# Decode attention of a hybrid decoder step: scores kept as groups of 32 partitions, transposes by VectorE, keys in transfers of 1.25 MB

## What is computed

```python
k_all = concatenate([kv_buf[:, :, 0], k], axis=1)          # 2048 cached rows and the 8 new ones
for _, d in ((128, 1), (512, 4), (2048, 16)):              # window, dilation
    idx = w_buf + arange(t)[:, None] - arange(129)[None, :] * d
    s = einsum('bthd,btkhd->bthk', q, k_all[:, idx]) * HEAD_DIM ** -0.5
    lse = logsumexp(s, axis=-1)
    outs.append(einsum('bthk,btkhd->bthd', exp(s - lse[..., None]), v_all[:, idx]))
# the three branches are weighted by the softmax of their lse
```

## Time and profile before

| | before |
|---|---|
| median of the runs | 1509.22 us |
| the profiled execution, its own time | 1509.26 us |
| its span, first to last instruction | 1507.3 us |
| PE busy | 1494.9 us |
| DVE busy | 824.6 us |
| ACT busy | 584.6 us |
| moved by DMA | 296.59 MB, mean 197 GB/s |
| attention of the new tokens | about 141 to 490 us |

### The profile page before, as it was taken

One profiled execution on the slowest core, in us unless ns is written; L12 is line 12 of the kernel. 1 busy time (PEld: TensorE's weight loads), 2 busy tenths in 40 slices (PEclk: granted clock), 3 DMA queues, 4 the chain that ended last, 5 costly groups with the idle time before them and its releaser, 6 DMA issues.

```text
span 1507.3 us, 27167 instructions
## 1 busy us (share of the span) xinstructions
PE 1494.9 (99%) x11095; PEld 1414.1 (94%) x11095; DVE 824.6 (55%) x1075; ACT 584.6 (39%) x792; POOL 221.7 (15%) x316
## 2 busy tenths in 40 slices
PE   9999999999999999999999999999999999999997
PEld 9999777777778999999999999999999999999997
DVE  7669899964566677444444444444444433333434
ACT  6333434446545354333333333333333323333332
POOL 7874344500630000000000000000000000000100
PEclk9999999999999999999999999999999999999999
DMA  7557899999987444444444444444444444444442
GB/s 270 187 160 246 293 370 371 335 367 356 345 316 263 155 149 145 154 153 144 150 153 147 146 153 150 144 151 153 145 148 153 147 147 153 152 143 153 150 151 105
DMA packets 83282, 296.59 MB, mean 197 GB/s; under 512 B 9984, under 2 KB 11136, under 8 KB 82816
## 3 DMA queue, kind: packets, MB, share of 16 engines
q1 hardware_dynamic: 82624, 294.34, 57.6%
q10 hardware_dynamic: 576, 1.08, 0.2%
HBM read 289.31 MB, written 5.43 MB: 196 GB/s over the span
## 4 chain that ended last, share of the span: by engine, by line
PE 90%; DVE 5%; POOL 2%; issue 1%; ACT 1%; DMA 0%; DVEq 0%; ACTq 0%
PE ps L2001 20%; PE ps L2002 20%; PE ps L2000 20%; PE ps L1846 6%; PE ps L1884 3%; PE ps L1848 3%; PE ps L1890 2%; PE ps L1885 2%; PE ps L1658 2%; PE ps L1687 2%; DVE wlo L986 1%; PE ps L1952 1%; PE ps L1953 1%; PE ps L1951 1%; POOL par L1425 1%
## 5 line engine op out<-in xcount | busy, mean ns | idle before, releaser
L1300 DVE TENSOR_TENSOR wlo<-raw,whi 128x1024 fp32r<-128x1024 f32 x264 | 325.2, 1232 | 519.9 <-ACT whi L863 519.8
L863 ACT ACTIVATE whi<-raw 128x1024 fp32r<-128x1024 f32 x264 | 279.9, 1060 | 606.2 <-PE ps L2002 601.7
L2002 PE MATMUL ps<-xh,wlo 128*128 128x320 f32 x1400 | 432.6, 309 | 0.0
L2000 PE MATMUL ps<-xh,whi 128*128 128x320 f32 x1400 | 432.6, 309 | 0.0
L2001 PE MATMUL ps<-xl,whi 128*128 128x320 f32 x1400 | 432.6, 309 | 0.0
L2000 PEld LDWEIGHTS ps<-xh,whi 128*128 128x128 f32 x1400 | 262.8, 188 | 0.0
L2002 PEld LDWEIGHTS ps<-xh,wlo 128*128 128x128 f32 x1400 | 262.8, 188 | 0.0
L2001 PEld LDWEIGHTS ps<-xl,whi 128*128 128x128 f32 x1400 | 262.8, 188 | 0.0
L2000 PE MATMUL ps<-hh,whi 128*128 128x320 f32 x696 | 215.1, 309 | 0.0
L2001 PE MATMUL ps<-hl,whi 128*128 128x320 f32 x696 | 215.1, 309 | 0.0
L2002 PE MATMUL ps<-hh,wlo 128*128 128x320 f32 x696 | 215.1, 309 | 0.0
(11 more groups left out here) (335 smaller groups left out, 1804.1 us busy)
## 6 DMA issues: line engine op xcount, KB each, us to landing
raw<-in_w_gu SPq DMA_DIRECT2D x176, 512.0 KB, 3.5
raw<-in_w_dn SPq DMA_DIRECT2D x88, 512.0 KB, 3.5
raw<-in_w_in SPq DMA_DIRECT2D x78, 512.0 KB, 5.9
kv<-in_ck SPq DMA_DIRECT2D x76, 512.0 KB, 6.7
kv<-in_cv SPq DMA_DIRECT2D x64, 512.0 KB, 7.7
raw<-in_w_out SPq DMA_DIRECT2D x32, 512.0 KB, 3.7
raw<-in_cv SPq DMA_DIRECT2D x16, 512.0 KB, 7.7
out_kv<-z SPq DMA_DIRECT2D x2, 1280.0 KB, 12.4
```

Of the source, the lines that this page charges most:

```text
L863: act.activation(whi[:, j % SPL, :], raw[:, j % RAW, :], ACT.Copy).then_inc(S["w_hi"], 1)
L1300: v.tensor_tensor(wlo[:, j % SPL, :], raw[:, j % RAW, :], whi[:, j % SPL, :].bitcast(F32), ALU.subtract) \
L2000: t_.matmul(out, whi[:, slot, w], ah[:, k, :], start=(k == 0), stop=False)
L2002: last = t_.matmul(out, wlo[:, slot, w], ah[:, k, :], start=False, stop=(k == 2 * units - 1))
```

## The change

The scores of a pair of head groups are kept as four groups of 32 partitions: partition group j holds the keys 32 j to 32 j + 31 of every tile of 128, and the free axis runs over four pairs of head groups (`sall` is 128 x 4 x 352). Four score steps replace five, one for each pair, each with 8 products of 320 columns whose keys lie in runs of 32. The new keys go to one partition group (8 products of 32 columns in one column group), and a memset keeps the others masked.

The maximum of a query now lies over four partition groups: ACT copies them side by side (`spread_maxima`, four copies), DVE reduces (`maxima`), ACT copies the result back (`spread_bias`, four copies), and the exponent is four instructions of 352 columns. The sums over the partition groups come from four one-column products on PE (`sum_probabilities`, bank 6) and DVE inverts them. The transposes of 32 x 32 blocks are one instruction on DVE (`turn_probabilities`), two for the first two batches; PE's transposes and ACT's evictions are gone.

A pair's keys are one load of 1.25 MB with rows of 2 KB, and the ring is laid out by size. Each batch starts one slot later, its values one step and its output one step earlier. GpSimd clears `vn` once at the start. The core of the diff:

```diff
-KEY_TILES = (KEYS_OLD + 512) // P
-NKEYS = KEY_TILES * P + DEC_BATCH * DEC_SEQ
+KEYS = KEYS_OLD + 512
+KEY_TILES = KEYS // P
+KQ = KEYS // 4
+KW = KQ + 32
 KU = 2 * P
-KN = KEY_TILES * P // KU
+KN = KEYS // KU
+KS = 4
+K_PARTS = ((0, KN),)
+NP = len(K_PARTS)
...
-START_OF = (36, 42, 48, 54, 60, 66, 72, 78)
-TURN, VALUES, OUTPUT = 5, 7, 12
+START_OF = (37, 43, 49, 55, 61, 67, 73, 79)
+TURN, VALUES, OUTPUT = 5, 6, 11
...
-        kv = upper.take("kv", [P, KV - 1, ATT_WIDTH])
+        kv = upper.take("kv", [P, KV_ROOM])
         hb_more = upper.take("hb_more", [P, 2, NT])
-        sall = upper.take("sall", [P, NKEYS])
-        ptk = upper.take("ptk", [P, KEY_TILES + 1, P])
+        sall = upper.take("sall", [P, 4, KW])
+        ptk = upper.take("ptk", [P, 4, KW])
...
-            for b in batches(s, TURN + 1):
-                end.append((7, ("pt", b, 2)))
-            for step in range(KN):
+            for step in range(KS):
                 for b in batches(s, step):
                     end.append((6, ("score", b, step)))
+            for b in batches(s, TURN):
+                end.append((6, ("norm", b)))
...
-                    "pt": lambda: ("pt_moved", 4 * key[1] + (key[2] + 1 if key[2] < 2 else 4)),
-                    "score": lambda: ("s_masked", 6 * key[1] + (key[2] + 1 if key[2] < 4 else 6)),
+                    "score": lambda: ("s_masked", KS * key[1] + key[2] + 1) if key[2] < KS - 1 else ("new_masked", key[1] + 1),
+                    "norm": lambda: ("s_sum", key[1] + 1),
...
+        KV_FROM, KV_AFTER, held, in_raw, pos = [], [], [], None, 0
+        for n, (kind, _, i) in enumerate(KV_ORDER):
+            size = kv_size(kind, i)
+            if kind == "v" and (in_raw is None or n - in_raw >= KV - 1):
+                KV_FROM.append(None)
+                KV_AFTER.append([] if in_raw is None else [in_raw])
+                in_raw = n
+                continue
+            if pos + size > KV_ROOM:
+                pos = 0
+            KV_AFTER.append([m for m, lo, hi in held if lo < pos + size and hi > pos])
+            held = [x for x in held if x[0] not in KV_AFTER[n]] + [(n, pos, pos + size)]
+            KV_FROM.append(pos)
+            pos += size
+        KV_DONE = []
+        for n in range(len(KV_ORDER)):
+            KV_DONE.append(max([KV_DONE[n - 1] if n else -1] + KV_AFTER[n]))
...
+                if kind == "k":
+                    c0, c1 = K_PARTS[i % NP]
+                    src = a["ck"][KN * b + c0:KN * b + c1, :, 512 * (i // NP):512 * (i // NP) + 512].rearrange("c p n -> p c n")
+                    sy.dma_start(kv_place(n).rearrange("p (c n) -> p c n", n=512), src).then_inc(KV_IN[n % KV], 16)
+                else:
+                    sy.dma_start(kv_place(n), a["cv"][KEY_TILES * b + i, :, :]).then_inc(KV_IN[n % KV], 16)
...
+            def spread_maxima(b):
+                act.wait_ge(S["s_max"], b + 1)
+                for j in range(4):
+                    act.activation(quads[0:32, j, :], smax[32 * j:32 * j + 32, 0:4], ACT.Copy).then_inc(S["s_spread"], 1)
+            def spread_bias(b):
+                act.wait_ge(S["s_top"], b + 1)
+                for j in range(4):
+                    act.activation(sbias[32 * j:32 * j + 32, 0:4], sbias[0:32, 4:8], ACT.Copy, scale=-SCALE).then_inc(S["s_bias"], 1)
             def exponent(b):
-                act.wait_ge(S["s_max"], b + 1)
-                act.activation(sall[:], sall[:], ACT.Exp, bias=smax[:, 7:8], scale=SCALE, accum_out=rsum[:, 0, b:b + 1]).then_inc(S["p_exp"], 1)
-            def probabilities(b, g):
-                act.wait_ge(S["pt_done"], 3 * b + g + 1)
-                if g == 0 and b:
-                    act.wait_ge(S["v_used"], KEY_TILES * b)
-                bank, w = (7 if g else 6), (4 if g < 2 else 2)
-                new = g == 2 and b >= LATE
-                act.activation(ptk[:, 4 * g:4 * g + w + new, :].rearrange("p a n -> p (a n)"), ps[:, bank, 0:(w + new) * P], ACT.Copy) \
-                    .then_inc(S["pt_moved"], 1 + new)
-                if g == 2 and b < LATE:
-                    if b == 0:
-                        act.wait_ge(S["x_rot"], PAIRED)
-                    act.activation(ptk_late[b][:], ps[:, bank, 256:384], ACT.Copy).then_inc(S["pt_moved"], 1)
+                act.wait_ge(S["s_bias"], 4 * b + 4)
+                for g in range(4):
+                    act.activation(sall[:, g, :], sall[:, g, :], ACT.Exp, bias=sbias[:, g:g + 1], scale=SCALE,
+                                   accum_out=psums[:, b, g:g + 1]).then_inc(S["p_exp"], 1)
...
-                for b in batches(s, TURN):
-                    probabilities(b, 0)
-                    probabilities(b, 1)
...
                 for b in batches(s, 4):
+                    spread_maxima(b)
+                    spread_bias(b)
                     exponent(b)
...
-                dve.wait_ge(S["k_used"], KN * b + i + 1)
-                m = max(i - 2, 0) * KU
-                v.tensor_tensor_reduce(out=sall[:, KU * i:KU * i + KU], in0=ps[:, 6, 0:KU], in1=mask[:, m:m + KU], scale=1.0, scalar=-3e38,
+                dve.wait_ge(S["k_used"], KS * b + i + 1)
+                v.tensor_tensor_reduce(out=sall[:, i, 0:KQ], in0=ps[:, 6, 0:KQ], in1=mask[:], scale=1.0, scalar=-3e38,
                                        op0=ALU.add, op1=ALU.max, accum_out=smax[:, i:i + 1]).then_inc(S["s_masked"], 1)
-                if i < KN - 1:
+                if i < KS - 1:
                     return
-                new = 8 * (DEC_BATCH - 1 - b)
-                v.tensor_tensor_reduce(out=sall[:, KEY_TILES * P:NKEYS], in0=ps[:, 6, KU:KU + 64], in1=mask_new[:, new:new + 64], scale=1.0,
-                                       scalar=-3e38, op0=ALU.add, op1=ALU.max, accum_out=smax[:, 5:6]).then_inc(S["s_masked"], 1)
-                dve.wait_ge(S["s_masked"], 6 * b + 6)
-                step(v.tensor_reduce(smax[:, 6:7], smax[:, 0:6], AX.X, ALU.max))
-                v.tensor_scalar(smax[:, 7:8], smax[:, 6:7], -SCALE, None, ALU.mult).then_inc(S["s_max"], 1)
+                own = slice(32 * (b // 4), 32 * (b // 4) + 32)
+                at = 8 * (DEC_BATCH - 1 - b)
+                valid = mask_new[own, at:at + 32].rearrange("p (a n) -> p a n", a=1).to_broadcast([32, 4, 32])
+                fresh = sall[own, :, KQ:KW]
+                if b:
+                    dve.wait_ge(S["new_masked"], b)
+                v.tensor_tensor(fresh, ps[own, 6, KQ:KQ + P].rearrange("p (a n) -> p a n", n=32), valid, ALU.add).then_inc(S["new_masked"], 1)
+                dve.wait_ge(S["new_masked"], b + 1)
+                step(v.tensor_reduce(smax[own, 4:8], fresh, AX.X, ALU.max))
+                dve.wait_ge(S["s_masked"], KS * b + KS)
+                v.tensor_tensor(smax[own, 0:4], smax[own, 0:4], smax[own, 4:8], ALU.max).then_inc(S["s_max"], 1)
+            def maxima(b):
+                dve.wait_ge(S["s_spread"], 4 * b + 4)
+                v.tensor_reduce(sbias[0:32, 4:8], quads[0:32].rearrange("p j g -> p g j"), AX.X, ALU.max).then_inc(S["s_top"], 1)
+            def no_new(quadrants):
+                for q in quadrants:
+                    step(v.memset(sall[q, :, KQ:KW], NEG))
+            def turn_probabilities(b):
+                dve.wait_ge(S["p_exp"], 4 * b + 4)
+                if b:
+                    dve.wait_ge(S["v_used"], KEY_TILES * b)
+                if b < LATE:
+                    if b == 0:
+                        dve.wait_ge(S["x_rot"], PAIRED)
+                    step(v.transpose(ptk_late[b][:], sall[:, :, KQ:KW]), wait=False)
+                v.transpose(ptk[:].rearrange("p a n -> p (a n)"), sall[:].rearrange("p a n -> p (a n)")).then_inc(S["p_turned"], 1)
+                dve.wait_ge(S["p_turned"], b + 1)
+                if b < DEC_BATCH - 1:
+                    no_new((slice(32, 64), slice(64, P)) if b + 1 < 4 else (slice(0, 32), slice(64, P)))
+            def inverse_sums(b):
+                dve.wait_ge(S["p_sums"], b + 1)
+                v.reciprocal(rsum[:, b:b + 1], ps[:, 6, 0:1]).then_inc(S["s_sum"], 1)
...
+                for b in batches(s, 4):
+                    maxima(b)
                 for b in batches(s, TURN):
-                    dve.wait_ge(S["p_exp"], b + 1)
-                    v.reciprocal(rsum[:, 1, b:b + 1], rsum[:, 0, b:b + 1]).then_inc(S["s_sum"], 1)
+                    turn_probabilities(b)
+                    inverse_sums(b)
...
+                if i == KS - 1:
+                    pe.wait_ge(S["z_done"], 20)
+                    q = slice(32 * (b // 4), 32 * (b // 4) + 32)
+                    for f in range(NF):
+                        at = KQ + 32 * (f // 2)
+                        t_.matmul(ps[q, 6, at:at + 32], qst[:, b % 2, f, :], z[:, ZK + f, SEQ + 32 * (b // 4):SEQ + 32 * (b // 4) + 32],
+                                  start=(f % 2 == 0), stop=(f % 2 == 1), tile_position=(0, 32 * (b // 4)))
+                for part, (c0, c1) in enumerate(K_PARTS):
```

(51 more changed lines are left out.)

122 lines of the change are left out of this document (65 added, 57 removed).

## The result

The changed kernel takes 1551.56 us (1550.57 to 1556.1) where the kernel before takes 1509.18 (the median of four): slower, ratio 1.0287, interval 1.0267 to 1.0308. The prediction was 1526 in 1507 to 1541: the sign was right, the time is above the range.

A forecast was written before the change was run, and what follows sets the result against it. PE, busy 99% of the span in its own order, was taken as the bound. PE's work -8 and new waits +25 gave +17 us on a 1507.3 span: span 1524.3, time 1526.2, range 1507 to 1541.

The forecast's parts named there:

- PE's own work: Products and transposes on PE: removed and added work sums to -0.93, say -1.0 us a batch, -8 us in all.
- The score step: On PE: four steps of 320 columns at 1.1 us replace five of 256; -0.05 us, nothing for the strided read.
- New keys: On PE, 16 records through one column group: 0.65 us a batch instead of 0.25, so +0.4.
- DVE's transpose: On DVE: one transpose of 1408 columns takes 1.65 us, from below 1.5 to twice that.
- The exponent: On ACT: cut into four of 352 columns, 0.57 us each, 2.3 together.
- The waits before the sums: End of slot 5: PE waits for the last of ACT's exponents, 15.4 us over the batches.
- The waits in slot 6: Slot 6: PE waits until DVE has inverted the sums and their bank is free, 14 us together.
- The discount: Both kinds of waits sum to 29 us; 25 taken, since a stall lets DVE catch up; ends 10 and 35.
- Transfers: Loads of keys and values: nothing on the path; 36.1 us of loading against a cycle of some 38.
- The rival: Loads decide in the cycles from 43 to 60: 4.3 us in three cycles on top, 1539; chance 0.13.
- The clock: On PE: every slice showed full clock before; a wait was priced at its full length, with no clock term.

The follow-up runs named there:

- e3: Changed kernel with keys laid out in memory so a transfer reads one 10 KB row per partition, not five of 2 KB; 1548.99 us, ratio 1.0268.
- e4: Kernel before, with ten stalls of PE alone, of different lengths, added in the last products (w_down); 1569.29 us, one execution.
- e1: Changed kernel with the products of the sums moved from the end of slot 5 to behind the last value tile; 1545.53 us, ratio 1.0246.
- e2: Changed kernel with filler products of 64 columns on constants put on PE where it stands before the sums; 1598.87 us.

## Why the prediction missed, step by step

**PE's own work** was predicted at -8 (the parts, -0.93 a batch, give -7.4) and is -9.0 by the balance. The score step takes 1.10 us, as said, so the read of keys in runs of 32 costs nothing. New keys took 0.50 us a batch, not 0.65. I had held the values equal; the block with the new values takes 1.43 us instead of 1.71, which I had not seen.

**DVE's transpose**: 1.630 us, predicted 1.65. **The exponent**: 0.577 each, predicted 0.57.

**The waits before the sums**: 15.4 predicted, 16.7 measured. By batch 4.2, 0.4, 3, 0.7, 0, 0, 2.5, 4.6 against 4.43, 0.86, 2.42, 2.10, 0, 0, 2.12, 4.74; only batch 3 is off. The chain of batch 7, ACT and DVE in the timeline:

```profile
492.96 2.15 DVE L996 RECIPROCAL rstd<-rtmp 128x320 f32<-128x320 f32 x1 [0.56 <-ACT rtmp L667]
493.19 0.87 ACT L722 ACTIVATE quads<-smax 32x4 f32<-32x4 f32 x4
495.15 0.17 DVE L1080 TENSOR_REDUCE sbias<-quads 32x4 f32<-32x16 f32 x1
495.36 0.89 ACT L728 ACTIVATE sbias<-sbias 32x4 f32<-32x4 f32 x4 [1.29 <-DVE sbias L1080]
496.26 1.28 ACT L733 ACT_TABLE_LOAD   x1
497.56 0.59 ACT L733 ACTIVATE sall<-sall,sbias 128x352 f32<-128x352 f32 x1
...
500.09 0.29 PE L1761 MATMUL ps<-psums,fold 128*32 128x1 f32 x8 [4.74 <-ACT sall L733]
```

Each step stands where the prediction put it: the reciprocal of the earlier trace rows ahead of the maxima, the copies, the table, the exponents, PE.

**The waits in slot 6**: 14 predicted, 12.6 measured, but partly for another reason. The bank of the sums has 4.5 of them, with a projection's wait for DVE's masks 5.2. The other 7.4 come from ACT and DVE being late for other things in their queues: the queries, the GLU's input, the prompt. I had looked only at who waits for the bank. By batch the waits are 0, 0.8, 1.7, 0.7, 2.0, 3.4, 3.9 and 0, against 0.7 to 1.0 in batches 0, 1 and 3, 2.5 in batch 2, 2 in each of 4 to 6 and 2.1 in batch 7 (these add up to 12.7 to 13.6, not 14). None came in batches 0 and 7, and behind both stalls the next unit ran at half clock, 5.0 us instead of 3.6 in batch 0; that this gave ACT and DVE the time is likely and not tested.

**The discount**: both kinds came to 29.4 in the prediction and are 29.3. I had taken 25, since a stall would let DVE catch up. In the sum it did not, so 4.3 us of the miss are this step. Batch 3, where I had 0.7, waited 2.1. That the two sums agree so closely is in part luck: the 2.8 to 3.1 us of slot 6 that stayed away in batches 0 and 7 are made up for by larger ones in batches 5 and 6.

**Transfers**: "nothing on the path, because PE has never waited for a load" was wrong, 9.1 us. The 38 us of a cycle were held against the rate of a full queue, and what counted was when a place comes free: a load released by one slot's products and wanted by the next slot's came late, and the queue stood empty before it (3 GB/s at 230 us). The rival had the place (one slot of lead) and not the mechanism: it put the price on rows of 2 KB, which e3 shows at 2.6 us at most, and its decision on a rate under 350 GB/s, where the queue had 370 when full.

**The clock** was not in the sum: 11.0 us, the largest part of the miss. Rows of before could not give it (every slice is 9), but the prediction foresaw waits of 4 to 5 us on an engine that had waited nowhere in the attention for more than 0.3 us, and priced them at their length alone. e4 shows that such a wait, alone, costs 1.5 us and more on top.

The miss of 25.0 us (span 1549.3 against 1524.3) is thus 11.0 of clock, 9.1 of loads, 4.3 of the discount, 1.6 of other small waits, less 1.0 of PE's own work. The steps that failed are the two terms put at nothing, the clock and the loads, and the discount; the chain that was forecast is there.

## What to carry to other kernels

Where one engine is busy 99% of the time, a step moved from it to others is worth its cycles only if nothing that it asks for comes later than before; list everything that stands behind the new work in those engines' queues, since moving the wait (e1) only finds the next of these. Count a stall of several microseconds there at more than its length, for the clock behind it. Of each load ask by which product its place is released and how many slots later it is wanted; a full queue's rate does not tell. And a slot of slack between a producer and its consumer may be worth more than the work that giving it up saves.

## What was not expected of the hardware

A stall of PE of 3.7 to 8.6 us between full-speed products was followed by half clock and cost 1.5 to 2.5 us on top; stalls of up to 3.1 us, alone, cost nothing more, yet in the attention waits of 1.98 to 2.42 us were followed by half clock too. Small products hold the clock and do not raise it: 15.7 us of them kept it at 1.00 in batch 0 of e2, and 17.0 us of PE, all busy, ran at 0.50 behind a wait of 2.10. At half clock a float32 product of 320 columns takes 0.267 us for 0.147, so 45% of the time is lost. A float32 product of 64 columns on a constant took 0.22 us (two records of 0.112) at full clock, nearly four times what I had taken. And with the keys in rows of 2 KB the queue had 370 GB/s against 388 with rows of 10 KB, with the queue's share worked out.
